# The value-table stage of a fused transformer layer on one Trainium2 core: whole chunks, the low half written over the raw chunk, gathered sums kept in PSUM

## The reference, cut to what matters

```
def tok_fn(args):
    xc, ec, gc = args                                    # 128 tokens; 8 heads x 16 experts each
    act = gelu(einsum('td,tkd->tk', xc, u[ec]))
    return einsum('tk,tkd->td', gc * act, v[ec])         # v: 16384 experts x 2048
```

## Time and profile before

| | us |
|---|---|
| median of 3 runs | 2115.66 (2112.12 to 2116.34) |
| the profiled execution | 2109.97 |
| its span | 2108.2 |
| TensorE busy (matmul) | 1363.5, 65% of the span |
| VectorE busy | 1522.7, 72% |
| ACT busy | 855.8, 41% |
| POOL busy | 831.2, 39% |
| bytes moved | 564.25 MB, mean 268 GB/s |

### The profile page before, as it was taken

One profiled execution on the slowest core, in us unless ns is written; L12 is line 12 of the kernel. 1 busy time (PEld: TensorE's weight loads), 2 busy tenths in 40 slices (PEclk: granted clock), 3 DMA queues, 4 the chain that ended last, 5 costly groups with the idle time before them and its releaser, 6 DMA issues.

```text
span 2108.2 us, 28409 instructions
## 1 busy us (share of the span) xinstructions
PE 1363.5 (65%) x8268; PEld 1191.7 (57%) x8268; DVE 1522.7 (72%) x2324; ACT 855.8 (41%) x1523; POOL 831.2 (39%) x1113
## 2 busy tenths in 40 slices
PE   6799999879896000000122112689989999999797
PEld 5799998779894000000122112576767777677597
DVE  4233433744445999999999999877777787778845
ACT  3233333643433001000676577544444444444432
POOL 1000100000005554555555453866666666666300
PEclk9899999989998555555555555999999999999898
DMA  8956545037356999999999999078888888887753
GB/s 216 248 179 187 182 128 160 1 114 226 123 182 274 417 410 406 413 394 413 414 404 405 410 414 415 6 254 280 275 274 281 272 286 281 274 283 282 243 168 112
DMA packets 184275, 564.25 MB, mean 268 GB/s; under 512 B 14277, under 2 KB 112870, under 8 KB 150177
## 3 DMA queue, kind: packets, MB, share of 16 engines
q0 software_dynamic: 59008, 341.95, 42.4%
q1 hardware_dynamic: 125216, 221.67, 31.9%
HBM read 556.23 MB, written 7.34 MB: 267 GB/s over the span
## 4 chain that ended last, share of the span: by engine, by line
PE 31%; DVE 27%; issue 16%; POOL 11%; DMA 11%; ACT 2%; POOLq 1%; DVEq 1%; SPq 0%; ACTq 0%
PE banks L1420 25%; DVE rows L1252 17%; POOL vrow L612 7%; DMA vrow<-peer_v_dram,vidx 5%; POOL vidx L609 3%; PE banks L1671 3%; DMA rows<-peer_u_dram,expert 2%; DMA raw<-w_in_dram 2%; DVE vlo L1320 1%; DVE xn L957 1%; DVE hres L1327 1%; POOL hot L632 1%; DMA wv_cmp<-cmp_wv_dram 1%; PE banks L1549 1%; DVE xtlo L964 0%
## 5 line engine op out<-in xcount | busy, mean ns | idle before, releaser
L1252 DVE SCALAR_TENSOR_TENSOR rows<-rows,banks 128x2048 f32<-128x2048 f32 x256 | 573.0, 2282 | 22.2 <-DMA rows<-peer_u_dram,expert 21.9
L917 ACT CAST vhi<-vraw 128x512 fp32r<-128x512 f32 x384 | 238.8, 622 | 320.4 <-PE banks L1671 279.0
L612 POOL DMA_INDIRECT vrow<-peer_v_dram,vidx x256 | 287.8, 1124 | 205.0 <-POOL vidx L609 147.4
L982 DVE TENSOR_TENSOR wlo<-raw,whi 128x2048 fp32r<-128x2048 f32 x77 | 177.1, 2300 | 264.4 <-ACT whi L667 264.4
L578 POOL DMA_INDIRECT rows<-peer_u_dram,expert x256 | 243.4, 951 | 279.0 <-DVE rows L1252 167.3
L1671 PE MATMUL banks<-vhi,chi 128*128 128x512 f32 x768 | 312.4, 407 | 49.1 <-DVE vlo L1320 47.1
L1420 PE MATMUL banks<-xthi,whi 128*128 128x256 f32 x1024 | 293.0, 286 | 13.9 <-DVE wlo L982 12.2
L1671 PE MATMUL banks<-vlo,chi 128*128 128x512 f32 x768 | 301.2, 392 | 0.0
L1671 PE MATMUL banks<-vhi,clo 128*128 128x512 f32 x768 | 300.9, 392 | 0.0
L1420 PE MATMUL banks<-xtlo,whi 128*128 128x256 f32 x1024 | 292.3, 285 | 0.0
L1420 PE MATMUL banks<-xthi,wlo 128*128 128x256 f32 x1024 | 292.1, 285 | 0.0
(11 more groups left out here) (217 smaller groups left out, 2547.8 us busy)
## 6 DMA issues: line engine op xcount, KB each, us to landing
vraw<-peer_v_dram SPq DMA_DIRECT2D x128, 768.0 KB
raw<-w_in_dram SPq DMA_DIRECT2D x48, 1024.0 KB, 5.4
raw<-w_out_dram SPq DMA_DIRECT2D x16, 1024.0 KB, 5.4
raw<-peer_wq_dram SPq DMA_DIRECT2D x16, 1024.0 KB, 5.3
raw<-ple_gate_dram SPq DMA_DIRECT2D x16, 1024.0 KB, 5.4
rows<-peer_u_dram,expert POOLq DMA_INDIRECT x256, 12.5
vrow<-peer_v_dram,vidx POOLq DMA_INDIRECT x256
bias_by_distance<-rvec POOLq DMA_DIRECT2D x1, 3072.0 KB, 36.3
```

The lines of the kernel that those rows point to most:

```text
L612: pool.indirect_dma_start(vrow[r][:, :], None, quarters, bass.IndirectOffsetOnAxis(ap=vidx[r][:, :], axis=0))\
L917: act.copy(vhi[b][:, :], vraw[r][:, b * VCOL:(b + 1) * VCOL]).then_inc(vhi_ready, 1)
L982: dve.tensor_tensor(wlo[r % 2][:, :, :], raw[r][:, :, :], whi[r % 2][:, :, :].bitcast(fp32), ALU.subtract).then_inc(lo_ready[stage], 1)
L1252: dve.scalar_tensor_tensor(out=r[:, :], in0=r[:, :], scalar=1.0, in1=xps[tt][:, :], op0=ALU.mult, op1=ALU.mult, accum_out=dots[b][:, k:k + ...
```

## The change

- A chunk's `vhi` is one ACT copy of 128x1536 (two buffers of 6 KB) and a chunk's `vlo` one VectorE subtraction of 128x1536, written over the raw chunk (`vlo[r]` has the address of `vraw[r]`). SP may therefore reload a chunk's buffer only when its low products are done, and no longer when its `vlo` is made. The ring still has four chunks. All loop bodies cover eight chunks (`VBODY`).
- TensorE takes a chunk's 12 products of `vhi` first (six with `chi`, six with `clo`) and then its six products of `vlo`. It counts two semaphores in place of `v_mm`: `v_hi_mm` and `v_lo_mm`.
- POOL copies eight indices at once (two tiles by four chunks, two index buffers) and then issues eight indirect DMAs, each after its own wait for a free row buffer and a `nop`. There are eight row buffers, as before.
- VectorE seeds PSUM banks 6 and 7 with the residual's last 512 columns, adds the gathered rows to those banks, one row of each token tile a chunk, and waits for the use two back. ACT copies the two banks back to `hres` at the end.

The diff, cut to its core:

```diff
-    vhi = [at(f"vhi{b}", (160 + 2 * b) * KB, [P, VCOL], f32r) for b in range(VUNITS)]
-    vlo = [at(f"vlo{b}", (166 + 2 * b) * KB, [P, VCOL], f32r) for b in range(VUNITS)]
+    vlo = [at(f"vlo{r}", (176 + 6 * r) * KB, [P, VBLK * VCOL], f32r) for r in range(VRING)]
+    vhi = [at(f"vhi{b}", (160 + 6 * b) * KB, [P, VBLK * VCOL], f32r) for b in range(2)]
...
+    v_sum = [bank[TT * VBLK + tt] for tt in range(TT)]
...
+            with sp.Fori(1, V_TURNS) as i:
+                for r in range(VBODY):
+                    sp.wait_ge(v_lo_mm, VBODY * i + r - VRING + 1)
+                    v_load(VBODY * i + r, r)
...
+            def v_fetch(i, half, first=False):
+
+                idx, count = vidx[half], VBODY // 2
+                c0 = VBODY * i + half * count
+                by_tile = slot_row[:, :].rearrange("p (t s) -> p t s", t=TT)
+                pool.tensor_copy(idx[:, :, :], by_tile[:, :, bass.ds(c0, count)]).then_inc(vidx_ready, 1)
+                pool.wait_ge(vidx_ready, 2 * i + half + 1)
+                pool.nop(nofuse=True)
+                for j in range(TT * count):
+                    if not first:
+                        pool.wait_ge(v_used, TT * c0 + j - VROWS + 1)
+                        pool.nop(nofuse=True)
+                    pool.indirect_dma_start(vrow[j][:, :], None, quarters,
+                                            bass.IndirectOffsetOnAxis(ap=idx[:, j % TT, j // TT:j // TT + 1], axis=0))\
+                        .then_inc(v_fetched[j], 16)
...
+                if not (peeled and r < 2):
+                    act.wait_ge(v_lo_mm, c - 1)
+                act.copy(chi[r % 2][:, :, :], spread[:, :, bass.ds(c, 1), :].rearrange("p a o t -> p a (o t)"))\
+                    .then_inc(chi_ready, 1)
+                act.wait_ge(v_landed[r % VRING], 16 * (VBODY // VRING * i + r // VRING + 1))
+                if not (peeled and r < 2):
+                    act.wait_ge(v_hi_mm, c - 1)
+                act.copy(vhi[r % 2][:, :], vraw[r % VRING][:, :]).then_inc(vhi_ready, 1)
...
+            for tt in range(TT):
+                act.wait_ge(v_used, TT * SLOTS - TT + tt + 1)
+                act.copy(hres[:, tt, VBLK * VCOL:D], v_sum[tt][:, :]).then_inc(peer_done, 1)
...
+            dve.wait_ge(spread_sb[1], SPREADS)
+            for tt in range(TT):
+                dve.tensor_copy(v_sum[tt][:, :], hres[:, tt, VBLK * VCOL:D]).then_inc(v_sums_set, 1)
+            dve.wait_ge(v_sums_set, TT)
...
+            def use_v_row(i, r, tt, peeled):
+
+                n = TT * r + tt
+                dve.wait_ge(v_fetched[n % VROWS], 16 * (TT * VBODY // VROWS * i + n // VROWS + 1))
+                if not (peeled and r == 0):
+                    dve.wait_ge(v_used, TT * VBODY * i + n - TT + 1)
+                dve.scalar_tensor_tensor(out=v_sum[tt][:, :], in0=vrow[n % VROWS][:, :],
+                                         scalar=slot_coef[:, bass.ds(VBODY * i + r + tt * SLOTS, 1)],
+                                         in1=v_sum[tt][:, :], op0=ALU.mult, op1=ALU.add).then_inc(v_used, 1)
...
+            def v_lows(i, r, peeled=False):
+
+                c = VBODY * i + r
+                dve.wait_ge(chi_ready, c + 1)
+                if not (peeled and r < 2):
+                    dve.wait_ge(v_hi_mm, c - 1)
+                dve.tensor_tensor(clo[r % 2][:, :, :], spread[:, :, bass.ds(c, 1), :].rearrange("p a o t -> p a (o t)"),
+                                  chi[r % 2][:, :, :].bitcast(fp32), ALU.subtract).then_inc(clo_ready, 1)
+                use_v_row(i, r, 0, peeled)
+                dve.wait_ge(vhi_ready, c + 1)
+                dve.tensor_tensor(vlo[r % VRING][:, :], vraw[r % VRING][:, :], vhi[r % 2][:, :].bitcast(fp32),
+                                  ALU.subtract).then_inc(vlo_ready, 1)
+                use_v_row(i, r, 1, peeled)
...
+            def v_products(i, r, first=False, final=False):
+
+                c = VBODY * i + r
+                pe.wait_ge(vhi_ready, c + 1)
+                for x in (chi[r % 2], clo[r % 2]):
+                    if x is clo[r % 2]:
+                        pe.wait_ge(clo_ready, c + 1)
+                    for tt in range(TT):
+                        for b in range(VBLK):
+                            last = pe.matmul(bank[tt * VBLK + b][:, :], x[:, tt, :],
+                                             vhi[r % 2][:, b * VCOL:(b + 1) * VCOL],
+                                             start=first and x is chi[0], stop=False, skip_group_check=True)
+                last.then_inc(v_hi_mm, 1)
+                pe.wait_ge(vlo_ready, c + 1)
+                for tt in range(TT):
+                    for b in range(VBLK):
+                        last = pe.matmul(bank[tt * VBLK + b][:, :], chi[r % 2][:, tt, :],
+                                         vlo[r % VRING][:, b * VCOL:(b + 1) * VCOL], start=False, stop=final,
+                                         skip_group_check=True)
+                last.then_inc(v_lo_mm, 1)
```

More of the change, by code:

```diff
@@ L277, in build @@
     idx4 = place("idx4", [P, TOKB])
-    vidx = [place(f"vidx{r}", [P, 1], i32) for r in range(GRING)]
+    vidx = [place(f"vidx{r}", [P, TT, VBODY // 2], i32) for r in range(2)]
     assert base + cursor[0] <= nc.sbuf_usable_end, (base + cursor[0], nc.sbuf_usable_end)
@@ L905, in _, with v_halves @@
             act.wait_ge(spread_sb[1], SPREADS)
[L906 to L921, removed]
-            act.wait_ge(peer_done, VBLK)
+            def v_halves(i, r, peeled=False):
+                c = VBODY * i + r
[7 more added lines that the diff above has]
+                act.copy(vhi[r % 2][:, :], vraw[r % VRING][:, :]).then_inc(vhi_ready, 1)
+            for r in range(VBODY):
+                v_halves(0, r, True)
+            with act.Fori(1, V_TURNS) as i:
+                for r in range(VBODY):
+                    v_halves(i, r)
+            for tt in range(TT):
+                act.wait_ge(v_used, TT * SLOTS - TT + tt + 1)
+                act.copy(hres[:, tt, VBLK * VCOL:D], v_sum[tt][:, :]).then_inc(peer_done, 1)
+            act.wait_ge(tile0_done, VBLK)
+            act.wait_ge(peer_done, TT)
             norm_sums("ple")
@@ L1338, in _ @@
+            for r in range(VBODY):
+                v_lows(0, r, True)
+            with dve.Fori(1, V_TURNS) as i:
+                for r in range(VBODY):
+                    v_lows(i, r)
+            dve.wait_ge(v_lo_mm, NKEYS)
+            for tt, done in enumerate((tile0_done, tile1_done)):
                 for b in range(VBLK):
                     cols = hres[:, tt, b * VCOL:(b + 1) * VCOL]
-                    dve.tensor_tensor(cols, cols, bank[tt * VBLK + b][:, :], ALU.add).then_inc(peer_done, 1)
@@ L1341, in _ @@
[L1341 removed]
+                    dve.tensor_tensor(cols, cols, bank[tt * VBLK + b][:, :], ALU.add).then_inc(done, 1)
+            dve.wait_ge(tile0_done, VBLK)
+            dve.wait_ge(tile1_done, VBLK)
+            dve.wait_ge(peer_done, TT)
             norm_and_split("ple", 2)
@@ L1659, in _ @@
                         spread_group(tt, i, m, False)
-            def v_products(i, first=False, final=False):
-                for r in range(VRING):
-                    c = VRING * i + r
-                    pe.wait_ge(clo_ready, c + 1)
-                    for b in range(VBLK):
-                        pe.wait_ge(vlo_ready, VBLK * c + b + 1)
-                        for tt in range(TT):
-                            hi, lo = chi[r % 2][:, tt, :], clo[r % 2][:, tt, :]
-                            for n, (x1, x2) in enumerate(((hi, vhi[b]), (hi, vlo[b]), (lo, vhi[b]))):
-                                last = pe.matmul(bank[tt * VBLK + b][:, :], x1, x2[:, :],
-                                                 start=first and r == 0 and n == 0,
-                                                 stop=final and r == VRING - 1 and n == 2, skip_group_check=True)
-                        last.then_inc(v_mm, 1)
@@ L1681, in _ @@
+            pe.wait_ge(spread_sb[1], SPREADS)
+            for r in range(VBODY):
+                v_products(0, r, first=r == 0)
+            with pe.Fori(1, V_TURNS - 1) as i:
+                for r in range(VBODY):
+                    v_products(i, r)
+            for r in range(VBODY):
+                v_products(V_TURNS - 1, r, final=r == VBODY - 1)
             transposes("ple")
```

76 lines of the change are left out of this document (20 added, 56 removed).

## The result

The changed kernel takes 2035.34 us (median of 4 runs, 2031.7 to 2042.34), the kernel before beside it 2113.89 us. The ratio is 0.9638, with a 95% interval of 0.9612 to 0.9664: 76.5 us less by the ratio, 78.6 by the two medians. The profiled execution took 2042.34 us with a span of 2040.6, against 2108.2 before, 67.6 less. Between 67.6 and 76.5 lie 9 us ahead of the stage, in code that the change does not touch: the stage's first matmul starts at 1375.56 us in the profile before and at 1384.73 in this one, and in the profiles of the experiments anywhere from 1375.7 to 1385.4.

The account below looks back on a forecast made before the run. POOL's serial copy, wait and issue (4.63 of 4.69 us a chunk) was the bound. With TensorE next, 523.9 us of steps, 1.7 slow start and 5 waits save 70 from the 2115.66 median: 2045 us, range 2035 to 2072.

Parts of the forecast that it names:

- first case: TensorE bounds the value-table stage: 2036 to 2056 us, by leftover waits of 0 to 15 us; chance 70%.
- the sum: Stage on TensorE: first matmul 1375.6, steps 523.9, slow start 1.7, leftover waits 5; VectorE's bank additions at 1906.7, not 1977.36.
- TensorE's step: In the value-table stage, matmuls start 0.2275 us apart; the same 18 make 4.10 us a chunk.
- The late last row: At the stage's end, the last gathered row lands behind the gate weights' loads; that 2.98 us wait ends.
- the cover named: Two seeding copies on VectorE (2 x 0.69 us) fit into its 5.50 us idle before the first `clo`; uncovered, 1.4 us.
- POOL's new price: One index copy, one wait, then eight gathers at 1.125 + 0.30 us each: 12.6 us, or 3.15 us a chunk.
- All three are under 4.10: POOL's estimate 3.15, upper bound 3.96 and lower bound 2.8 us a chunk all lie below TensorE's 4.10.
- POOL stays the bound: Rival, 4%: `vlo` subtractions of 1.76 us each hold POOL up; 4.54 us a chunk, 19 saved, 2097 us.
- VectorE's time with two SBUF inputs falls: With gathered sums in PSUM, VectorE's instructions with two SBUF inputs fall from 4.0 to 2.2 us a chunk.
- SP's added wait: Chunk reload waits for the low products; holds TensorE up only if landing time L, taken as 6 to 8, exceeds 10.4 us.
- the loop: Refill of the chunk ring: one turn takes landing time L + 6.0 us, so with four chunks (L + 6.0)/4 a chunk.
- TensorE's clock: Rival, 2%: the clock falls to 1.2 GHz; low for a quarter of the stage, 5.1 us a chunk, 2170 us.

## Why the prediction was right, point by point

The forecast was 2045 us, 70.7 saved, in a range of 2035 to 2072; measured were 2035.34 and 76.5 to 78.6 saved. That is inside the range by 0.3 us only, and below the 2036 to 2056 of its first case. Of the 10 us between forecast and measurement, 5.8 are terms of the sum (below), 1.8 come from the kernel before, whose median beside this one was 2113.89 and not 2115.66, and the rest is no more than runs of one kernel differ by (2031.7 to 2042.34). The low end was not worked out: with no leftover waits at all the prediction's own sum gives 2040.7, and 2035 comes out of it only against the profiled execution, the base that it had set aside. So the mechanism was right, and that the range held was in part luck.

- **What bounds the kernel before**: POOL's serial chain. Shown by two runs, one that shortened only that chain (68 us gained) and one that took 174 us from TensorE (7 us gained).
- **TensorE's step**: right. 4.10 us a chunk forecast, 4.08 measured.
- **The sum**: from first matmul to the additions it has 531.1 us; 525.3 were measured. The term that was mis-sized is "for what is left of waits I take 5 us": it is nil, since TensorE ran 450.00 us in 450. The step of 0.2267 in place of 0.2275 took off another 1.9. The slow start took more: the first 18 matmuls needed 6.93 us (1384.73 to 1391.66) in place of 4.08, so 2.9 and not 1.7. In the profiles of nine of the ten experiments the same 18 took 5.6 to 5.8 us, which is 1.5 to 1.7.
- **The late last row**: right, the wait is gone.
- **VectorE and ACT**: right. `vlo` 1.762 us (1.76 forecast), the row use 0.748 (0.75, of bounds from 0.64 to 1.31), `vhi` 1.476 (about 1.5). The two seeding copies cost nothing, but not by the cover named: they wait for the last of `spread`, which is also what ends VectorE's idle time, and took 1.29 us (1382.81 to 1384.09) while TensorE waited for `vhi` until 1384.73.
- **POOL's new price**: wrong in size. Forecast was 1.125 us a DMA instruction, at most 1.494; it is 1.581, at most 2.53. POOL's busy time and waits fill the window, and it waits only 8.5 us for buffers where the prediction looked for such waits. Eight gathers take 15.9 us (363.8 us busy and 77.9 of waits other than for buffers, for 222 gathers) where 12.6 were forecast: 3.98 us a chunk, over the prediction's bound from above of 3.96. "All three are under 4.10" thus came true by 0.1 us, and that was luck; it cost no time only because TensorE needs 4.08 us. The rival "POOL stays the bound" had the right mechanism; at 3.71 us a chunk, in the run with fewer products, it begins to show. Nor is the price fixed: in that run the mean is 1.42 us.
- **"VectorE's time with two SBUF inputs falls"** was offered against that rival. It is true and worth nothing (the run with the sums in SBUF): a row use in SBUF does hold POOL up, but in that run only 27 of 197 DMA instructions begin in one, and 96 in the long subtraction.
- **SP's added wait**: L was taken as 6 to 8 us; 5.8 us came out of the ring of two by the loop, 5.2 by the timeline. The limit was 10.4.
- **The DMA engines**: 320 GB/s at a share of 0.94 forecast, 322 at 0.92 measured, and 351 were possible.
- **TensorE's clock** stayed at 1.00 from 1400 us on, with a bank change at every matmul. That rival did not come about.

## What to carry to other kernels

An engine can set the pace at 65% busy when its work is a serial chain of copy, semaphore and issue: multiply the whole cycle by its count before trusting shares, and batch the small copy in it. One part of the change, the index copies, brought most of its gain; the other parts bring little, and without it they lose. When a VectorE instruction with two SBUF inputs is made longer, look at what POOL issues beside it: it costs nothing until POOL is the bound.

## What the runs showed of the hardware that was not expected

- A DMA instruction on POOL that begins during a 1.76 us subtraction of two SBUF tensors ends about 0.8 us after it, up to 2.53 us in all, against 0.94 undisturbed. One that begins in an instruction of 2.28 us with one input in SBUF and one in PSUM takes 0.94 as well.
- Matmuls of 128x512 that change the bank every time started 0.2267 us apart, each of 1765 steps from 1400 to 1800 us between 0.226 and 0.228; with three in a row into one bank, and another order of the halves, 0.2280 on average, the steps between 0.224 and 0.240.
- After some 50 us of small matmuls with gaps, the last of them 3.1 us, the first chunk of the stage runs partly at TensorE's lower clock. From 1384 to 1392 us the granted clock is 0.59:

```profile
1384.00:1392.00 8.00, 7.27 (x20) 5.81 (x21) 6.83 (x9) 2.41 (x4) 6.01 (x6) 0.59 0.62 171
```

- The same instructions ahead of the stage end up to 10 us apart from one profile to another (1375.6 to 1385.4 us for the first matmul). A comparison of two profiles by their spans carries that.
